# First block's input projections as three single-pass products, with lead-in, expert end and query scaling rearranged

## The chip, the core and the metric

The kernel runs on one core of a Trainium2 chip. The metric is the device time of one execution in microseconds. The engines of the core run side by side, each with its own list of instructions, and wait for each other by semaphores: TensorE (PE in the rows, its weight loads PEld), VectorE (DVE), ScalarE (ACT), GpSimd (POOL), and SyncE (SP), which only issues transfers from memory.

## What is computed

Two blocks of two layers each, over 256 tokens of width 1024, all in float32. Of the reference the first block matters most, cut here to the lines around the change:

```python
h = rmsnorm(x, ln1_g[i]) @ w_in[i]
(fq, fk, fv, ff, dq, dk, dv, c_q, c_kv, k_r) = jnp.split(h, split_points, axis=-1)
o_fox = fox_group(fq, fk, fv, ff, fgate_b[i])
o_diff = diff_group(dq, dk, dv, lam_q1[i], lam_k1[i], lam_q2[i], lam_k2[i], diff_norm_g[i], lam_init)
o_mla = mla_group(c_q, c_kv, k_r, q_norm_g[i], w_uq[i], kv_norm_g[i], w_ukv[i], pos)
x = x + jnp.concatenate([o_fox, o_diff, o_mla], axis=-1) @ w_o[i]
up = causal_dwconv(rmsnorm(x, ln2_g[i]) @ w_up[i], conv_w[i], conv_b[i])
...
q2 = jax.nn.silu(to_heads_2(hq, HGRN_HEADS)) * (HGRN_HEAD_DIM ** -0.5)
...
return jax.vmap(lambda yb, ib: jnp.zeros((s, d), yb.dtype).at[ib.reshape(-1)].add(yb.reshape(-1, d)))(ye, idx)
```

`w_in[i]` is 1024 by 2724. The second block has a mixer of retention and HGRN2 heads (whose queries are `q2`) and sixteen experts of width 1024, and the experts' outputs are added back to their tokens (last line).

## The kernel before, in words

**First block, a layer (loop over `lay`, TensorE from line 1754 on).** The normalised rows are transposed on TensorE (`turn_normed`) into PSUM and copied out to `XT` with the gain. The projection is cut into twelve blocks (`IN_BLOCKS`): `cq`, `ckv`, `dq0`, `dk0`, `dv0`, then `dq1`, `dk1`, `dv1`, `fv`, `ff`, `fq`, `fk`, all 256 columns wide except `ckv` (160: 128 as `tokens_product`, 32 as `columns_product`) and `ff` (4). Each block has two halves of eight products over the 1024 inputs. Weights come from memory through a ring of six slots of 1 MB (`load` at line 747, in the order of use); a slot is given back by `release`, which runs one block late: it waits for the last block's `proj` when the next one is released. Blocks 0 to 4 run with the small latent and MLA products between them. Blocks 5 to 11 stand in a loop of six turns (`n`, `N_SHARED`): half a block, `step(2n)`, half a block, `step(2n+1)`. A step is the scores of one head's unit, the transposes of the unit before and the values of the one before that; between these VectorE adds the bias and takes the minimum (L1373), ScalarE does the exponential (L1015) and copies the transposes (L1022), VectorE scales the outputs (L1385 to L1399).

**The products.** A float32 product of the language is two matrix instructions in the trace. The feed-forward part (`up`, `down`) already works in another way: a weight tile is rounded by ScalarE into `W1` (`split_round`, L726), VectorE writes the remainder into `W2` (`split_rest`, L730), the rows are split likewise into `XT1` and `XT2`, and each product is three instructions of one pass, `W1·XT1`, `W1·XT2`, `W2·XT1` (L1988 to L1990, L2001), with three pairs of buffers. The first two feed-forward tiles are rounded behind the last attention unit. `split_rest` of the second one stands in VectorE's list between the first and the second of the four additions to the residual (L1436). Its slot is that of `fk`, which the late `release` gives back only when the output projection's first slot is released.

**The lead-in.** SyncE issues the load of `X` and of the identity and then waits for all the small parameter rows before it loads weights. ScalarE issues these rows (17 transfers, L949), waits for the lambda dots, issues the first table of constants, loads its function table and then does the squares of the first norm (L602). VectorE does the lambda dots and the parameter copies first, and the second block's lower bounds behind the first transposes. TensorE turns the parameter rows, does 20 idle products on the identity (L1734) and then the transposes and block 0.

**Second block.** `hqT`, the queries of 128 by 1024, is scaled by GpSimd (L872) once both halves are in; GpSimd then does the level exponents (L888, L889), which all levels of the scores need. In the experts, four groups of four, TensorE waits for each quad of weights (L2200). At a group's end ScalarE copies the left half of the outputs, VectorE the right one, and four products (L2238) scatter both halves to the tokens, followed by four additions (L1699) and, behind the last group, the squares of the next norm (L602). Of the last quad the right halves are loaded last.

## Time and profile before

| | us |
|---|---|
| median of 3 runs | 2084.36 (2083.1 to 2088.19) |
| the profiled execution, its own time | 2084.47 |
| its span in the profile | 2082.7 |
| PE busy | 1675.8 (80% of the span) |
| DVE busy | 620.8 (30%) |
| ACT busy | 449.5 (22%) |
| POOL busy | 176.6 (8%) |

The profile is of one execution. The first block's layer 0 lies at 0 to about 374 us, layer 1 up to 734, the second block's layers from there to about 1406 and to the end. The busy shares are means over stages: in the expert stages, from about 970 us and from about 1640 us on, the transfers move 421 GB/s nearly throughout, while in the first block they move at most 241 GB/s in any fortieth up to 728 us.

### The profile page before, as it was taken

The page shows a single profiled execution, that of the slowest core. Times are in us where ns is not written, and L with a number is a line of the kernel's source. Part 1 is how long each engine was busy: PE and PEld are TensorE (multiplying, and loading weights), DVE is VectorE, ACT ScalarE, POOL GpSimd, SP SyncE. Part 2 cuts the span into 40 slices and gives each one's busy share as a digit, 9 for nine tenths or more (in the row PEclk, how much of TensorE's full clock was granted, in tenths as well). Part 3 has the DMA queues.
Part 4 walks back from the last instruction along what each step waited for, and adds up shares of the span by engine and source line. Part 5 has one row for each costly group of instructions (what it writes and reads, how often), then busy time and mean ns, then how long its engine had stood idle before and what let it go on. Part 6 is the DMA issues. An engine that isn't in the chain of part 4 may idle for free.

```text
span 2082.7 us, 24357 instructions
## 1 busy us (share of the span) xinstructions
PE 1675.8 (80%) x10076; PEld 1165.3 (56%) x10076; DVE 620.8 (30%) x1067; ACT 449.5 (22%) x827; POOL 176.6 (8%) x129
## 2 busy tenths in 40 slices
PE   7999999999999999997565656569999665565665
PEld 6788999788899888983121212118888221121211
DVE  1235666232666665522000000006632110000001
ACT  1244544123455442211000000004212000000000
POOL 0010000001000017410000000002731000000000
PEclk9999999999999999998787788789999788788868
DMA  7226555231655573348999999999234899999997
GB/s 241 90 67 203 190 190 179 74 102 47 233 184 190 173 238 112 115 161 340 421 421 421 421 421 421 421 397 287 95 135 198 337 421 422 421 421 422 421 421 281
DMA packets 197426, 559.94 MB, mean 269 GB/s; under 512 B 15240, under 2 KB 137526, under 8 KB 148934
## 3 DMA queue, kind: packets, MB, share of 16 engines
q1 hardware_dynamic: 187616, 549.82, 68.9%
q10 hardware_dynamic: 9702, 8.57, 1.3%
q8 instruction: 82, 1.34, 0.3%
q14 instruction: 26, 0.21, 0.0%
HBM read 557.30 MB, written 1.05 MB: 268 GB/s over the span
## 4 chain that ended last, share of the span: by engine, by line
PE 50%; issue 24%; DMA 16%; DVE 4%; PEld 2%; ACT 2%; POOL 1%; SPq 1%; ACTq 0%; PEldq 0%; DVEq 0%; POOLq 0%; another core or an unknown queue 0%
DMA ring<-in_w_down 9%; PE psum L1749 8%; PE psum L1741 8%; PE psum L2001 5%; PE psum L2200 5%; PE psum L1988 4%; PE psum L1989 4%; PE psum L1990 4%; DMA ring<-in_w_up 4%; DMA ring<-in_w_gate 3%; PE psum L2111 3%; PE psum L2068 2%; PEld psum L1919 1%; PE psum L1869 1%; PE psum L634 1%
## 5 line engine op out<-in xcount | busy, mean ns | idle before, releaser
L2200 PE MATMUL psum<-ring,arena 128*32 128x512 f32 x2960 | 479.1, 798 | 325.4 <-DMA ring<-in_w_down 133.0
L2200 PEld LDWEIGHTS psum<-ring,arena 128*32 128x32 f32 x2960 | 114.2, 140 | 663.7 <-issue 655.1
L1741 PE MATMUL psum<-XT,ring 128*128 128x256 f32 (+1 forms) x1056 | 234.2, 381 | 0.0
L1741 PEld LDWEIGHTS psum<-XT,ring 128*128 128x128 f32 (+1 forms) x1056 | 196.5, 188 | 30.9 <-issue 2.4
L1988 PE MATMUL psum<-XT,W 128*128 128x256 f32 x704 | 200.0, 284 | 0.1
L1989 PE MATMUL psum<-XT,W 128*128 128x256 f32 x704 | 199.4, 283 | 0.0
L1990 PE MATMUL psum<-XT,W 128*128 128x256 f32 x704 | 199.3, 283 | 0.0
L730 DVE TENSOR_TENSOR W<-ring,W 128x2048 fp32r<-128x2048 f32 x66 | 151.2, 2290 | 106.8 <-ACT W L726 106.8
L1749 PE MATMUL psum<-ring,XT 128*128 128x256 f32 (+1 forms) x832 | 177.1, 371 | 0.0
L1749 PEld LDWEIGHTS psum<-ring,XT 128*128 128x128 f32 x832 | 152.1, 190 | 19.9 <-issue 0.8
L1692 DVE TENSOR_TENSOR arena<-arena,psum 128x512 f32<-128x512 f32 x16 | 11.0, 689 | 467.7 <-PE psum L2200 467.7
L726 ACT ACTIVATE W<-ring 128x2048 fp32r<-128x2048 f32 x66 | 124.2, 1908 | 85.0 <-PE psum L1990 58.3
L1988 PEld LDWEIGHTS psum<-XT,W 128*128 128x128 f32 x704 | 134.2, 191 | 1.0 <-DVE XT L707 0.3
L1989 PEld LDWEIGHTS psum<-XT,W 128*128 128x128 f32 x704 | 134.2, 191 | 0.8
L1990 PEld LDWEIGHTS psum<-XT,W 128*128 128x128 f32 x704 | 134.2, 191 | 0.0
L2001 PE MATMUL psum<-W,hT 128*128 128x512 f32 x528 | 128.1, 399 | 4.6 <-DVE hT L1464 4.6
L2001 PEld LDWEIGHTS psum<-W,hT 128*128 128x128 f32 x528 | 100.0, 192 | 26.4 <-DVE hT L1464 5.5
L1694 DVE COPY arena<-psum 128x512 f32<-128x512 f32 x8 | 5.5, 692 | 315.4 <-PE psum L2200 315.4
L621 POOL TENSOR_TENSOR arena<-arena 128x2 f32<-128x2 f32 x8 | 5.6, 697 | 817.1 <-DVE arena L613 817.1
L1454 DVE SCALAR_TENSOR_TENSOR arena<-psum,arena 128x255 f32<-128x255 f32 (+1 forms) x176 | 72.6, 476 | 3.8 <-ACT arena L1083 3.0
L1222 ACT ACTIVATE arena<-psum 128x512 f32<-128x512 f32 x16 | 9.6, 598 | 290.7 <-PE psum L2227 289.7
L1225 ACT ACTIVATE arena<-psum 128x512 f32<-128x512 f32 x8 | 4.8, 598 | 284.1 <-PE psum L2200 284.1
(253 smaller groups left out, 1742.7 us busy)
## 6 DMA issues: line engine op xcount, KB each, us to landing
ring<-in_w_up SPq DMA_DIRECT2D x170, 1024.0 KB, 17.1
ring<-in_w_down SPq DMA_DIRECT2D x142, 1024.0 KB, 19.4
ring<-in_w_gate SPq DMA_DIRECT2D x116, 1024.0 KB, 18.4
ring<-in_w_in SPq DMA_DIRECT2D x56, 1024.0 KB, 6.5
arena<-in_w_gate SPq DMA_DIRECT2D x12, 1024.0 KB, 12.6
ring<-in_w_o SPq DMA_DIRECT2D x8, 1024.0 KB, 5.2
ring<-in_w_out SPq DMA_DIRECT2D x8, 1024.0 KB, 5.2
ring<-in_w_down SPq DMA_DIRECT2D x16, 512.0 KB, 15.3
```

What stands on the lines that cost most here:

```text
L726: nc.scalar.activation(W1[(v - FF_USE) % W_BUFS][:, :], slot(s), ACT.Copy).then_inc(rounded, 1)
L730: nc.vector.tensor_tensor(W2[(v - FF_USE) % W_BUFS][:, :], slot(v % SLOTS_1), W1[(v - FF_USE) % W_BUFS][:, :].bitcast(F32), ALU.subtract). ...
L1454: last = nc.vector.scalar_tensor_tensor(out=dst, in0=psum[:, 4 + 2 * (j % 2) + g, m * S:m * S + S - tap], scalar=par[:, col + c:col + c + ...
L1741: last = nc.tensor.matmul(out, wt[:, k, c0:c0 + m], XT[:, k, :], start=(k == 0), stop=(k == KD - 1))
L1749: last = nc.tensor.matmul(out, XT[:, k, t * P:(t + 1) * P], wt[:, k, c0:c0 + n], start=(k == 0), stop=(k == KD - 1))
L1988: nc.tensor.matmul(dst, w1[:, k, c], XT1[:, k, :], start=(k == 0), stop=False)
L1989: nc.tensor.matmul(dst, w1[:, k, c], XT2[:, k, :], start=False, stop=False)
L1990: last = nc.tensor.matmul(dst, w2[:, k, c], XT1[:, k, :], start=False, stop=(k == KD - 1))
L2001: last = nc.tensor.matmul(psum[:, 2 * t + c, :], a, b[:, m, 512 * c:512 * (c + 1)], start=(j == 0 and m == 0 and b is w1 and a is h1), sto ...
L2068: last = nc.tensor.matmul(psum[:, 2 * (l % 2) + i, h * P:(h + 1) * P], lk[:, h, i * P:(i + 1) * P], lq[:, h, j * P:(j + 1) * P], start=Tru ...
L2111: last = nc.tensor.matmul(psum[:, 4 + i, t * S:(t + 1) * S], XT[:, k, t * P:(t + 1) * P], wt[:, k, :], start=(t == 0 and k == 4), stop=(k ...
L2200: last = nc.tensor.matmul(psum[CAP * e:CAP * (e + 1), bank + c, :], src[:, 2 * pair + k, CAP * e:CAP * (e + 1)], tiles[e][:, k, 512 * c:51 ...
```

## The change

**Projections.** The twelve blocks of both layers are now computed as the feed-forward part already was: `split_round` on ScalarE, `split_rest` on VectorE, and three single-pass products (`tokens_of`, `columns_of`), with two pairs of buffers in turn (`split_pair`). A tile may be rounded once the block two before it is done (`proj`). A slot of the ring is given back at the start of its block (`split_ready`). The 32 rope columns of `ckv` are computed as the last 32 of 96 columns. In layer 1 the first two tiles are split at the end of layer 0.

**Lead-in.** Twelve parameter rows are issued half by SyncE and half by ScalarE; SyncE doesn't wait for them before the weights. ScalarE loads its table first and does the squares as soon as `X` is there; the five lambda rows are issued behind the squares, the table of constants behind the transposes. The lambda and lower bound work moves behind block 4's splits on VectorE. TensorE does no idle products in layer 0.

**Second block.** ScalarE scales each half of the queries itself. In each layer's last expert group ScalarE copies both halves of the outputs; the left half is scattered before TensorE waits for the last weights, and the additions and squares go by halves.

```diff
+SPLIT_IN = 11
+SPLIT_ORDER = list(range(6)) + ["ff"] + list(range(6, SPLIT_IN)) + list(range(FF_USE, USES_1))
+SPLIT_AT = {v: n for n, v in enumerate(SPLIT_ORDER)}
...
+def split_pair(v):
+
+    return v % 2 if v < SPLIT_IN else (v - FF_USE) % 3
...
-            nc.scalar.activation(W1[(v - FF_USE) % W_BUFS][:, :], slot(s), ACT.Copy).then_inc(rounded, 1)
+            elif v >= FF_USE:
+                act.wait_ge(proj, past(proj) + block_of(SPLIT_IN - 1 - (v - FF_USE)) + 1)
+            elif v >= 2:
+                act.wait_ge(proj, past(proj) + block_of(v - 2) + 1)
+            elif past(up_mm):
+                read, k = ((up_mm, 0), (down_mm, 1))[v]
+                act.wait_ge(read, past(read) - k)
+            n = split_width(v)
+            nc.scalar.activation(W1[split_pair(v)][:, 0:n], slot(s, n), ACT.Copy).then_inc(rounded, 1)
...
+            sp.wait_ge(s_zero, 5)
+            for dst, src in parameter_rows()[1::2]:
+                sp.dma_start(dst, src).then_inc(s_rows, 16)
...
-            sp.wait_ge(s_rows, ROWS)
...
-                pool.wait_ge(emp_act, past(emp_act) + 6)
-                pool.tensor_scalar(hqT, hqT, HD ** -0.5, None, ALU.mult).then_inc(hq_scaled, 1)
...
+            nc.scalar.preload_act_table_set(EXP_LN_SET)
+            for dst, src in parameter_rows()[0::2]:
                 act.dma_start(dst, src).then_inc(s_rows, 16)
-            act.wait_ge(s_lamd, 2 * DEPTH)
-            act.dma_start(cst[:, P:], const1[:, P:]).then_inc(s_tables, 16)
-            nc.scalar.preload_act_table_set(EXP_LN_SET)
-            nc.scalar.activation(lame, lams, ACT.Exp).then_inc(s_lame, 1)
+            act.wait_ge(s_small, SMALL)
+            squares(act, BY_ROWS, None, sumsq)
+            for dst, src in lambda_rows():
+                act.dma_start(dst, src).then_inc(s_lamr, 16)
...
+                scale_last_tokens(act, past, 0)
+                act.wait_ge(s_par, 2 * (lay + 1))
                 if lay == 0:
-                    act.wait_ge(par_cur, 1)
-                    squares(act, BY_ROWS, None, sumsq)
-                else:
-                    squares(act, BY_ROWS, lambda i: (x_out, past(x_out) - 3 + i), sumsq)
-                act.wait_ge(par_cur, past(par_cur) + 1)
-                scale_last_tokens(act, past, 0)
-                turn_act(act, past, 0, par[:, C_LN1:C_LN1 + 8])
+                    split_round(act, past, 0)
+                turn_split_act(act, past, 0, 0, par[:, C_LN1:C_LN1 + 8])
+                if lay == 0:
+                    split_round(act, past, 1)
...
+                    act.dma_start(cst[:, P:], const1[:, P:]).then_inc(s_tables, 16)
...
+                split_round(act, past, 2)
...
+                split_round(act, past, 3)
...
+                split_round(act, past, 4)
...
+                split_round(act, past, 5)
+                if lay == 0:
+                    act.wait_ge(s_lamd, 2 * DEPTH)
+                    nc.scalar.activation(lame, lams, ACT.Exp).then_inc(s_lame, 1)
+                    act.wait_ge(set2, 2)
+                    nc.scalar.activation(lb_t[:, 8:16], lb_t[:, 8:16], ACT.Exp).then_inc(set2a, 1)
+                act.wait_ge(wu_loaded, past(wu_loaded) + 48)
+                nc.scalar.activation(wf1[:, :, :], wf, ACT.Copy).then_inc(rounded, 1)
...
+                    if n < N_SHARED - 1:
+                        split_round(act, past, 6 + n)
...
+                if lay < DEPTH - 1:
+                    for v in range(2):
+                        split_round(act, before(lay + 1), v)
...
+                    if name[:2] == "hq":
+                        act.wait_ge(emp_act, past(emp_act) + n + 1)
+                        nc.scalar.activation(dst, dst, ACT.Copy, scale=HD ** -0.5).then_inc(hq_scaled, 1)
...
-                    act.wait_ge(dn_mm, past(dn_mm) + 1)
-                    nc.scalar.activation(YE[:, 0:512], psum[:, 6, :], ACT.Copy).then_inc(ye_ready, 1)
+                    for c in range(2 if g == N_GROUPS - 1 else 1):
+                        act.wait_ge(dn_mm, past(dn_mm) + c + 1)
+                        nc.scalar.activation(YE[:, 512 * c:512 * (c + 1)], psum[:, 6 + c, :], ACT.Copy).then_inc(ye_ready, 1)
...
-                nc.vector.tensor_copy(par, par_all[:, lay, :]).then_inc(par_cur, 1)
-                dve.wait_ge(par_cur, past(par_cur) + 1)
+                par = par_all[:, lay, :]
+                if lay == 0:
+                    dve.wait_ge(s_small, SMALL)
                 norm_dve(dve, past, 0)
-                turn_dve(dve, past, 0, par[:, C_LN1:C_LN1 + 8])
                 if lay == 0:
-                    lower_bounds()
+                    parameters()
+                turn_split_dve(dve, past, 0, 0, par[:, C_LN1:C_LN1 + 8],
+                               (lambda: split_rest(dve, past, 0)) if lay == 0 else None)
+                if lay == 0:
+                    split_rest(dve, past, 1)
+                split_rest(dve, past, 2)
...
+                split_rest(dve, past, 3)
                 dve.wait_ge(latT, past(latT) + 1)
...
+                split_rest(dve, past, 4)
                 copied_by_dve(3, dkT[:, 0:2, :])
...
+                split_rest(dve, past, 5)
+                if lay == 0:
+                    lambdas()
+                    lower_bounds()
+                dve.wait_ge(rounded, past(rounded) + SPLIT_AT["ff"] + 1)
+                nc.vector.tensor_tensor(wf2[:, :, :], wf, wf1[:, :, :].bitcast(F32), ALU.subtract).then_inc(rest, 1)
...
+                    if n < N_SHARED - 1:
+                        split_rest(dve, past, 6 + n)
                     bias_and_max(2 * n)
...
+                    for n, (t, cols, c) in enumerate(BY_ROWS if g < N_GROUPS - 1 else BY_HALVES):
+                        dve.wait_ge(sc_mm, past(sc_mm) + n + 1)
+                        nc.vector.tensor_tensor(X[:, t, cols], psum[:, scatter_bank(g, t, c), :], X[:, t, cols], ALU.add).then_inc(x_moe, 1)
...
-                idle_products(7, IDLE_PRODUCTS["first block"])
+                if lay:
+                    idle_products(7, IDLE_PRODUCTS["first block"])
...
+                def split_ready(v):
+
+                    pe.wait_ge(rest, past(rest) + SPLIT_AT[v] + 1)
+                    pe.sem_inc(slot_free[v % SLOTS_1], 1)
+                    return W1[split_pair(v)][:, :], W2[split_pair(v)][:, :]
+
+                def columns_of(out, w1, w2, c0, m):
+
+                    for k in range(KD):
+                        c = slice(c0, c0 + m)
+                        nc.tensor.matmul(out, w1[:, k, c], XT1[:, k, :], start=(k == 0), stop=False)
+                        nc.tensor.matmul(out, w1[:, k, c], XT2[:, k, :], start=False, stop=False)
+                        last = nc.tensor.matmul(out, w2[:, k, c], XT1[:, k, :], start=False, stop=(k == KD - 1))
+                    return last
+
+                def tokens_of(out, t, w1, w2, n, fresh=False):
+
+                    rows = slice(t * P, (t + 1) * P)
+                    for k in range(KD):
+                        if fresh:
+                            pe.wait_ge(xt_rest, past(xt_rest) + k + 1)
+                        nc.tensor.matmul(out, XT1[:, k, rows], w1[:, k, 0:n], start=(k == 0), stop=False)
+                        nc.tensor.matmul(out, XT1[:, k, rows], w2[:, k, 0:n], start=False, stop=False)
+                        last = nc.tensor.matmul(out, XT2[:, k, rows], w1[:, k, 0:n], start=False, stop=(k == KD - 1))
+                    return last
 
...
-                        last = tokens_product(b[:, half * P:(half + 1) * P], half, wt, 0, KV_RANK)
+                        last = tokens_of(b[:, half * P:(half + 1) * P], half, w1, w2, KV_RANK)
                         if half:
-                            last = columns_product(b[NOPE:MLA_QK, S:2 * S], wt, KV_RANK, ROPE)
+                            last = columns_of(b[0:MLA_QK, S:2 * S], w1, w2, KV_RANK - NOPE, MLA_QK)
...
-                        if name != "ff":
-                            release(proj, past(proj) + i + 1, [use(i) % SLOTS_1])
...
+                                scatter(0, BY_HALVES[:TT])
...
+                    def scatter(half, chunks):
+                        pe.wait_ge(ye_ready, past(ye_ready) + half + 1)
+                        for t, cols, c in chunks:
+                            nc.tensor.matmul(psum[:, scatter_bank(g, t, c), :], GT[:, g, t * P:(t + 1) * P], YE[:, cols],
+                                             start=True, stop=True).then_inc(sc_mm, 1)
...
+                    if g < N_GROUPS - 1:
+                        scatter(1, BY_ROWS)
+                    else:
+                        scatter(1, BY_HALVES[TT:])
```

The lead-in in ScalarE's list: before, the issues are followed by the constants, the table and the squares. (L949 are the parameter and lambda rows, L951 the constants, L602 the squares, L609 the scaling of the last tokens, L663 the transposed rows.)

```order
L949 DMA arena<-in_lam_q 128x2x64
L949 DMA arena<-in_lam_k 128x2x64
L949 DMA arena<-in_lam_q 128x2x64
L949 DMA arena<-in_lam_k 128x2x64
L951 DMA arena<-first_constants 128x2912
L952 ACT_TABLE_LOAD
L953 ACTIVATE arena<-arena 128x4
L602 ACTIVATE XN,arena<-X 128x512 x4
L609 ACTIVATE XN<-X,arena 128x512 x2
L663 ACTIVATE XT<-psum,arena 128x256 x4
```

And in the changed kernel (L645 squares, L995 lambda rows, L652 scaling, L779 the rounding, L737 the rows' first parts):

```order
L991 DMA arena<-in_fgate_b 1x2x4
L991 DMA arena<-in_norm_g 8x2x128
L645 ACTIVATE XN,arena<-X 128x512 x4
L995 DMA arena<-in_diff_norm_g 128x2x128
L995 DMA arena<-in_lam_q 128x2x64
L995 DMA arena<-in_lam_k 128x2x64
L995 DMA arena<-in_lam_q 128x2x64
L995 DMA arena<-in_lam_k 128x2x64
L652 ACTIVATE XN<-X,arena 128x512 x2
L765 ISA
L779 ACTIVATE W_0_49<-ring 128x2048
L737 ACTIVATE XT_55<-psum,arena 128x256 x6
```

The table and half of the rows stand ahead of the squares, the five lambda rows between squares and scaling, and the rounding of the first tile ahead of the turned rows' first parts.

VectorE between block 1 and the MLA copies, before (L1309, L1312 and L1314 empty the latents and the rope columns, L1317 and L1321 are the turned latents, L1305 the copy of `dk0`):

```order
L1309 TENSOR_SCALAR arena<-psum,arena 128x256 x2
L1312 TENSOR_SCALAR arena<-psum,arena 128x128 x2
L1314 COPY arena<-psum 32x256
L1317 TENSOR_TENSOR arena<-psum,arena 128x512
L1321 TENSOR_SCALAR arena<-psum,arena 128x256
L1305 COPY arena<-psum 128x512
L1327 COPY arena<-psum 64x512 x2
```

And in the changed kernel (L784 is `split_rest`, L1382 to L1387 the latents and the rope columns, L1391 and L1395 the turned latents, L1378 the copy of `dk0`):

```order
L784 TENSOR_TENSOR W_0_52<-ring,W_0_49 128x2048
L1382 TENSOR_SCALAR arena<-psum,arena 128x256 x2
L1385 TENSOR_SCALAR arena<-psum,arena 128x128 x2
L1387 COPY arena<-psum 32x256
L784 TENSOR_TENSOR W_1_53<-ring,W_1_50 128x2048
L1391 TENSOR_TENSOR arena<-psum,arena 128x512
L1395 TENSOR_SCALAR arena<-psum,arena 128x256
L784 TENSOR_TENSOR W_0_52<-ring,W_0_49 128x2048
L1378 COPY arena<-psum 128x512
L1402 COPY arena<-psum 64x512 x2
```

The remainder of the tile of `dk0` now stands behind the latents, whose squares wait for block 1, and that of `dv0` behind the turned latents.

GpSimd in the second block's mixer, before (L869 limits the forget terms, L872 scales the queries, L888 and L889 are the exponents of the first level):

```order
L869 TENSOR_SCALAR arena<-arena 128x512 x4
L872 TENSOR_SCALAR arena<-arena 128x1024
L888 TENSOR_TENSOR arena<-arena 128x4x128
L889 TENSOR_TENSOR arena<-arena 128x4x128
L888 TENSOR_TENSOR arena<-arena 128x8x64
```

And in the changed kernel:

```order
L927 TENSOR_SCALAR arena<-arena 128x512 x4
L943 TENSOR_TENSOR arena<-arena 128x4x128
L944 TENSOR_TENSOR arena<-arena 128x4x128
L943 TENSOR_TENSOR arena<-arena 128x8x64
L944 TENSOR_TENSOR arena<-arena 128x8x64
```

The scaling is gone from the list, and the exponents follow at once.

## Rows read from the trace of the kernel before

**Rows 1.** The page: the span, and the chain that ended last by engine.

```profile
span 2082.7 us, 24357 instructions
PE 50%; issue 24%; DMA 16%; DVE 4%; PEld 2%; ACT 2%; POOL 1%; SPq 1%; ACTq 0%; PEldq 0%; DVEq 0%; POOLq 0%; another core or an unknown queue 0%
```

**Rows 2.** Windows: stretch, length, busy us (count) per engine, clock, DMA share, GB/s.

```profile
68.00:150.00 82.00, 81.32 (x445) 66.94 (x444) 27.33 (x112) 29.17 (x105) 6.38 (x6) 1.00 0.27 81
```

**Rows 3.** Timeline, lead-in: start, us, engine, line, operation, tiles, count, [idle before].

```profile
13.45 6.81 PE L1734 MATMUL psum<-arena 128*128 128x128 f32 x40
17.34 0.63 ACT L602 ACTIVATE XN<-X 128x512 f32<-128x512 f32 x1 [1.75 <-DVE arena L1296]
23.76 10.64 PE L1749 MATMUL psum<-ring,XT 128*128 128x256 f32 x64
34.33 10.74 PE L1741 MATMUL psum<-XT,ring 128*32 128x256 f32 x48
```

**Rows 4.** DMA issues (KB, us to landing); one issue on ScalarE in the timeline.

```profile
X<-in_x SPq DMA_DIRECT2D x1, 1024.0 KB, 4.9
...
8.97 0.49 ACTq L949 DMA_DIRECT2D arena<-in_lam_k  x1
```

**Rows 5.** Timeline: neighbouring single-pass products; chain of waits: 24 products 512 wide.

```profile
185.18 0.28 PE L1990 MATMUL psum<-XT,W 128*128 128x256 f32 x1
185.30 0.28 PE L1988 MATMUL psum<-XT,W 128*128 128x256 f32 x1
...
205.26 5.49 PE psum L2001 x24
```

**Rows 6.** The page's groups: line, operation, count | busy, mean ns | idle.

```profile
L730 DVE TENSOR_TENSOR W<-ring,W 128x2048 fp32r<-128x2048 f32 x66 | 151.2, 2290 | 106.8 <-ACT W L726 106.8
L726 ACT ACTIVATE W<-ring 128x2048 fp32r<-128x2048 f32 x66 | 124.2, 1908 | 85.0 <-PE psum L1990 58.3
```

**Rows 7.** Timeline, third and fourth block of layer 0 and the latents between them.

```profile
38.41 0.28 ACT L989 ACTIVATE arena<-psum 128x128 f32<-128x128 f32 x1
41.94 0.42 DVE L1314 COPY arena<-psum 32x256 f32<-32x256 f32 x1
45.57 7.07 PE L1741 MATMUL psum<-XT,ring 128*128 128x256 f32 x32
```

**Rows 8.** Timeline, attention steps of layer 0: two half blocks one step apart.

```profile
77.55 3.62 PE L1741 MATMUL psum<-XT,ring 128*128 128x256 f32 x16
83.00 3.62 PE L1741 MATMUL psum<-XT,ring 128*128 128x256 f32 x16
```

**Rows 9.** Timeline, from the output projection to the second norm, layer 0.

```profile
163.78 9.66 PE L1919 MATMUL psum<-ring,XT 128*128 128x256 f32 x44
164.88 5.66 SPq L752 DMA_DIRECT2D ring<-in_w_up  x3
172.00 2.29 DVE L730 TENSOR_TENSOR W<-ring,W 128x2048 fp32r<-128x2048 f32 x1 [3.01 <-ACT W L726]
177.90 0.16 DVE L613 TENSOR_REDUCE arena<-arena 128x2 f32<-128x10 f32 x1 [1.82 <-ACT XN L602]
```

**Rows 10.** Timeline, second block's mixer, layer 0, around the query scaling.

```profile
785.01 0.69 DVE L1557 TENSOR_TENSOR arena<-arena 128x512 f32<-128x512 f32 x1
785.15 3.18 POOL L872 TENSOR_SCALAR arena<-arena 128x1024 f32<-128x1024 f32 x1 [8.80 <-ACT arena L1148]
796.49 3.56 PE L2068 MATMUL psum<-arena 128*128 128x128 f32 x16 [5.14 <-POOL arena L896]
```

**Rows 11.** Timeline, the end of the last expert group.

```profile
2066.12 3.54 PE L2200 MATMUL psum<-ring,arena 128*32 128x512 f32 x16 [3.12 <-DMA ring<-in_w_down]
2070.57 3.71 PE L2238 MATMUL psum<-arena 128*128 128x512 f32 x8 [0.90 <-DVE arena L1694]
2075.04 0.63 ACT L602 ACTIVATE XN<-X 128x512 f32<-128x512 f32 x1
```

**Rows 12.** Timeline, last down projection of layer 0's feed-forward part.

```profile
366.17 7.42 PE L2001 MATMUL psum<-W,hT 128*128 128x512 f32 x24 [2.31 <-DVE hT L1464]
```

265 lines of the change are left out of this document (136 added, 129 removed).

## Prediction

> **What bounds the kernel now.** The page's chain gives TensorE half of the span and transfers 16% [rows 1]; the windows say where. In the attention loop of layer 0 TensorE is busy 81.3 of 82 us, VectorE 27.3 and ScalarE 29.2 [rows 2]. So the first block is TensorE's, with room on the two engines that would split the weights. The expert stages wait for transfers and are not touched but at their ends; what the stages ahead save moves them forward unchanged. I therefore read the timeline of the first block product by product, and then each place where the change moves something.
>
> **Price of a product.** A whole block of 256 columns is 16 products, 32 instructions in 7.07 us [rows 7]; the last one's tail overlaps, so it takes about 6.9, a half about 3.45. Single-pass instructions start 0.12 us apart [rows 5], so a block will be 48 x 0.12 = 5.76. Gain 1.14 for each of ten blocks. `ff` has 8 products and gains 0.57.
>
> `ckv` is open. Before, cq and ckv's 128-column products take 10.64 together [rows 3], so these take 3.57, or 0.22 a product; with the 32 rope columns (3.45) 7.0. After, the rope part costs 24 x 0.12 = 2.9. No row shows a single-pass product 128 wide. From below: 24 products 512 wide take 5.49 [rows 5], 0.229 each, so 256 columns more cost 0.109, and 128 less would give 0.066. From above: as much as the whole float32 product of that width, 0.22. I take 0.12, that of the nearest row of its kind, since the same 128x128 weights are loaded for each. Then the block is 48 x 0.12 + 2.9 = 8.6, a loss of 1.6; the ends are 6.1 (gain 0.9) and 13.5 (loss 6.5). The Trainium skill's page TensorE: Matmul & The Clock Gate, section LDWEIGHTS, has a load take columns/1.2 ns, 107 ns for 128; by it the block would be about 8.0. No row shows a load alone.
>
> **Splitting, where it lies.** A tile costs ScalarE 1.91 and VectorE 2.29 [rows 6]. *In the loop*, a turn is two half blocks and two steps; the half blocks start 5.45 apart [rows 8], so a turn is 10.9 before and 10.9 - 1.14 = 9.8 after. Before, ScalarE is busy 29.17/82 of it and VectorE 27.33/82 [rows 2], 3.9 and 3.6 a turn; with the splits [rows 6] it is 5.8 and 5.9 of 9.8. More than the sums count the places. I laid the two lists against TensorE's (an estimate, to some 0.5): rounding ends 3.4 into the turn, the remainder at 5.7, two bias operations and the exponential of unit 2n at 7.8, and its transposes are due at 8.5. So nothing waits, by 0.7. The turn of `ff` adds the forget gate to ScalarE ahead of the rounding: I count 0.8 lost. Five turns: 5 x 1.14 + 0.57 - 0.8 = 5.5 gained a layer.
>
> *At the fourth block* it is on the path. Its tile can be rounded only when block 1 is done (two pairs), the latents' squares follow, GpSimd's power, VectorE's latents, and only then stands its `split_rest`. Chain from block 1's end: rounding 1.9, from the squares to the end of VectorE's rope copy 42.36 - 38.0 = 4.4 [rows 7], remainder 2.3, with handovers 8.8. Block 2 and the latents' transposes are 5.8 + 1.0. So block 3 starts about 2 us late, and from block 0's end to its own end there are 8.6 + 8.8 + 5.8 = 23.2, against (45.57 - 30.9) + 6.9 = 21.6: a loss of 1.6 a layer, against 1.1 that the sum of products alone would give. With the ends for `ckv` it is a gain of 0.9 or a loss of 6.5.
>
> *From there to the loop's second turn* block 4 and block 5 gain 2.3. In layer 0 the lambda work and the lower bounds (some 5 us of small operations with two waits on ScalarE) now stand on VectorE between block 5's remainder and the MLA rotations; with the next remainder behind them the first bias comes late, and I count 1.7 of waiting: gain 0.6 there, 2.3 in layer 1. Block 0 of layer 1 gains 1.0; its tiles are split behind the last down projection, 7.42 us on TensorE [rows 12], which hides 3.1 and 3.7 us; without it they would cost that.
>
> **Second norm.** Before, `fk`'s slot comes back at 164.88, the weight lands 5 us later, is rounded and its remainder ends at 174.3, with three additions behind it; the sums are reduced at 177.90 [rows 9]. Given back at `fk`'s start, the tile is there long before. Next late is TensorE: its last product ends at 173.4 [rows 9]; addition, squares and handover bring the reduction to 175.3. Gain 2.6 a layer.
>
> **Lead-in.** The squares start at 17.34, block 0 at 23.76, ends at 30.9 [rows 3]. `X` lands 4.9 after its issue [rows 4], so the squares run from 6.2 to 8.7. Five issues of 0.49 [rows 4] hold ScalarE until 11.2; scaling ends at 12.6, the rounding of tile 0 at 14.6 (its load is issued near 5 and lands at 10 to 12), remainder at 17.1, where block 0 starts. TensorE has done nothing but transposes. Before, its first 20-odd idle instructions ran at half pace: 40 took 6.81 against 0.11 each later [rows 3], so some 2.4 us were lost where nothing waited. Now that loss falls on block 0: end 17.1 + 5.8 + 2.3 = 25.2. Gain 5.5, between 3 and 7. The Trainium skill's page TensorE: Matmul & The Clock Gate, section PE-mode transpose, says that transposes don't bring the full clock; that speaks against dropping the idle products, and the 2.3 stand with or without it.
>
> **Query scaling.** GpSimd's 3.18 delays the first exponents; they could start at 785.7 behind VectorE's last key instead of 788.4, and TensorE waits 5.14 for what follows [rows 10]. Gain 2.6 in each of two layers. ScalarE's two scalings lie under the blocks that TensorE still has.
>
> **Expert end.** The last weights land at 2066.12, scatter starts at 2070.57, the last square at 2075.04 [rows 11]. The left half's copy, scatter and addition now fit into TensorE's wait before 2066.12. Behind the last weights two scatters and two additions are left: last square at about 73.3. Gain 1.75, twice.
>
> **Sum.** Lead-in 5.5. Layer 0: -1.6 + 0.6 + 5.5 + 2.6 = 7.1. Layer 1: 1.0 - 1.6 + 2.3 + 5.5 + 2.6 = 9.8. Scaling 5.2, expert ends 3.5. Together 31.1. One price more: where TensorE waited 2.31 before the last down projection, 24 products took 7.42 instead of 5.49 [rows 12], 1.9 lost. There are three or four new waits of about 2 us; I take one such loss, 2 us. Gain 29. The profiled execution's own time is 2084.47, 1.8 over its span and 0.1 over the median 2084.36: 2084.5 - 29 = **2055.5**.
>
> **Rivals.**
> - *Narrow products at the float32 price* (0.22): 4.9 more a layer, and no wait of block 3 hides it, since its chain begins at block 1's end. 2055.5 + 9.8 = 2065. For it: half of the float32 cost here is columns, and nothing shows the single-pass form keeping its pace below 256. Against: 512 and 256 lie on one line.
> - *Narrow products at 0.066*: 2.5 less a layer, 2050.5.
> - *The lead-in doesn't move*: if tile 0 lands late behind `X` and the rows, or the cold start lasts longer, its 5.5 are gone: 2061.
> - *Slower: the splits end on the path in the loop.* If ScalarE and VectorE can't run ahead of TensorE, each of twelve turns shows 1.91 + 2.29 = 4.2: 50 us, 2106. It decides at 29/12 = 2.4 exposed per turn; I find 0.7 us of room instead, and VectorE is a third busy today [rows 2]. Partly exposed, at 2 us a turn, it would be 2080, about no change.
>
> **Chances.** Main case (2051 to 2060) 0.45; narrow products at 0.22 (2061 to 2070) 0.32; at 0.066 (2046 to 2051) 0.1; lead-in not moved, alone, 0.06; no change 0.04; slower 0.03. The range 2047 to 2069 leaves out under 2 in 10. A measurement here tells 0.3% (6 us) from no change: faster 0.93, same 0.04, slower 0.03.
>
> **What would show it.** Right: block 0's first product near 17 and its end near 25; single-pass products 0.12 apart in all blocks; TensorE waiting 2 us before block 3 and none in the loop; the reduction of the second norm 2 behind the output projection; GpSimd's exponents right behind the last key; one copy and two scatters behind the last weights. Wrong: ckv's 48 narrow products taking 10 us and not 6; a wait on `split_rest` in any turn; block 0 later than 19. The forecast falls if the loop's turn is not near 9.8.

## The result and the profile after the change

The changed kernel takes 2038.21 us (median of 4 runs, 2036.06 to 2038.32) against 2083.83 (4 runs, 2083.1 to 2088.19): 0.9774 of the time before, 95% interval 0.9757 to 0.9791. That is 46 us less, where I had forecast 29: the direction was right, the gain was more than half as large again, and 2038 lies under the range's lower end of 2047.

The page of the profile after answers to [rows 1]: span, busy times, chain by engine.

```profile
span 2036.3 us, 25114 instructions
...
PE 1644.7 (81%) x10420; PEld 1158.6 (57%) x10420; DVE 678.1 (33%) x1103; ACT 492.1 (24%) x861; POOL 175.4 (9%) x127
...
PE 45%; issue 24%; DMA 17%; PEld 6%; DVE 5%; ACT 2%; POOL 1%; SPq 1%; PEldq 0%; ACTq 0%; DVEq 0%; POOLq 0%; another core or an unknown queue 0%
```

TensorE's share of the chain fell from 50% to 45% of a shorter span, with 10420 instructions instead of 10076: more instructions, but shorter ones. VectorE is busy 33% of the span (30 before) and ScalarE 24% (22): the price of splitting, and it lies beside TensorE's work.

I followed the same instruction through both traces, place by place. "Ahead" is before minus after; "gained" is what the stretch up to that place adds to it; the last column is the term that the prediction had for it.

| place | before | after | ahead | gained | forecast |
|---|---|---|---|---|---|
| block 1 starts (end of lead-in and block 0) | 30.8 | 23.2 | 7.6 | 7.6 | 5.5 |
| block 3 done, MLA products start | 52.5 | 45.9 | 6.6 | -1.0 | -1.6 |
| loop's second turn starts | 77.6 | 69.7 | 7.9 | 1.4 | 0.6 |
| first unit behind the loop | 134.7 | 120.0 | 14.6 | 6.7 | 5.5 |
| second norm turned, first feed-forward product | 181.7 | 164.4 | 17.3 | 2.7 | 2.6 |
| layer 1: block 0 starts | 380.7 | 363.5 | 17.2 | -0.1 | 0 |
| block 3 done | 409.4 | 392.3 | 17.1 | -0.1 | -0.6 |
| loop's second turn starts | 434.5 | 414.9 | 19.5 | 2.4 | 2.3 |
| turning the mixed heads behind the loop | 494.2 | 467.9 | 26.3 | 6.7 | 5.5 |
| second norm turned | 539.4 | 509.7 | 29.8 | 3.5 | 2.6 |
| mixer of layer 0: first product | 743.0 | 713.4 | 29.6 | -0.2 | 0 |
| first level scores | 796.5 | 763.2 | 33.3 | 3.7 | 2.6 |
| behind the levels | 893.8 | 859.3 | 34.5 | 1.2 | 0 |
| last 16 expert products of layer 0 | 1396.9 | 1362.7 | 34.1 | -0.4 | 0 |
| mixer of layer 1: first product | 1410.4 | 1372.9 | 37.5 | 3.4 | 1.75 |
| first level scores | 1463.8 | 1423.1 | 40.7 | 3.2 | 2.6 |
| behind the levels | 1561.9 | 1519.2 | 42.8 | 2.1 | 0 |
| last 16 expert products of layer 1 | 2066.1 | 2023.2 | 42.9 | 0.1 | 0 |
| reduction of the last norm | 2075.9 | 2029.5 | 46.4 | 3.5 | 1.75 |

The forecast terms add up to 31.1, the measured ones to 46.4; the forecast then took off 2 us for a slower clock behind new waits, of which this profile shows nothing. So 17.3 us were missing, and they are spread: some 5 in the mixers, 3.4 at the expert ends, 2.1 in the lead-in, 2.4 in the two loops, 2 that were not lost, and smaller ones.

**Lead-in.** Timeline of the changed kernel (start, us, engine, line, operation, tiles, count, idle before); it answers to [rows 3, 4].

```profile
6.17 0.63 ACT L645 ACTIVATE XN<-X 128x512 f32<-128x512 f32 x1 [3.27 <-DMA arena<-first_constants]
6.19 0.41 ACTq L995 DMA_DIRECT2D arena<-in_diff_norm_g  x1
...
8.38 0.51 ACTq L995 DMA_DIRECT2D arena<-in_lam_k  x1
...
9.88 1.34 ACT L652 ACTIVATE XN<-X,arena 128x512 f32<-128x512 f32 x2 [1.16 <-POOL arena L664]
...
10.74 3.65 PE L677 MATMUL psum<-arena,XN 128*128 128x128 f32 x16 [1.20 <-ACT XN L652]
11.66 1.91 ACT L779 ACTIVATE W<-ring 128x2048 fp32r<-128x2048 f32 x1 [0.45 <-DMA ring<-in_w_in]
...
13.61 2.29 DVE L784 TENSOR_TENSOR W<-ring,W 128x2048 fp32r<-128x2048 f32 x1
...
16.00 0.55 PE L1868 MATMUL psum<-W,XT 128*128 128x256 f32 x1 [1.61 <-issue]
...
23.19 0.22 PE L1868 MATMUL psum<-W,XT 128*128 128x128 f32 x1
```

The squares stand at 6.17 as I expected. The five lambda issues are on ScalarE's queue from 6.19 to 8.9, beside its squares and not ahead of its next work. So the scaling starts at 9.88, when GpSimd's power is there, and the chain goes on with the rounding at 11.66 (it waits 0.45 for the tile's load) and the remainder at 13.61. Block 0 starts at 16.00 and is done at 23.19.

**The narrow products and the fourth block.** Timeline, TensorE, end of block 1 to block 3; it answers to [rows 3, 7].

```profile
28.39 0.28 PE L1870 MATMUL psum<-W,XT 128*128 128x128 f32 x1
28.50 0.30 PE L1857 MATMUL psum<-XT,W 128*96 128x256 f32 x1
...
31.36 0.28 PE L1857 MATMUL psum<-XT,W 128*128 128x256 f32 x1
...
37.70 0.67 PE L1907 MATMUL psum<-arena 128*128 128x128 f32 x4 [0.44 <-DVE arena L1387]
...
40.11 0.36 PE L1857 MATMUL psum<-XT,W 128*128 128x256 f32 x1 [1.53 <-DVE W L784]
```

From 23.19 to 28.50 stand the 48 single-pass products (one instruction each) with 128 moving columns: 0.111 each. The rope part takes 28.50 to 31.36, 2.9. Block 1 takes 8.2. Block 3 waits 1.53 for VectorE's remainder (L784).

**The loop.** Windows (stretch, length, busy us and count of PE, PEld, DVE, ACT, POOL, then clock, DMA share, GB/s): three turns of layer 1.

```profile
414.93:444.17 29.24, 29.24 (x226) 26.45 (x224) 15.81 (x47) 14.37 (x35) 0.00 (x0) 1.00 0.31 106
```

A turn is 29.24 / 3 = 9.75 us against 10.9 [rows 8], TensorE is never idle in it, VectorE is busy 5.3 us of it and ScalarE 4.8.

**The waits that are left, and the second norm.** Timeline, TensorE: the first exponential of layer 0's loop, and the transposes of the second norm in both layers.

```profile
69.38 0.52 PE L1989 MATMUL psum<-arena 128*128 128x128 f32 x3 [1.02 <-ACT arena L1069]
...
162.44 1.96 PE L677 MATMUL psum<-arena,XN 128*128 128x128 f32 x16 [0.55 <-ACT XN L652]
...
507.72 1.96 PE L677 MATMUL psum<-arena,XN 128*128 128x128 f32 x16 [0.55 <-ACT XN L652]
```

The same transposes in the kernel before:

```profile
179.74 1.94 PE L634 MATMUL psum<-arena,XN 128*128 128x128 f32 x16 [3.24 <-ACT XN L609]
...
536.30 3.14 PE L634 MATMUL psum<-arena,XN 128*128 128x128 f32 x16 [2.88 <-ACT XN L609]
```

The waits of 3.24 and 2.88 became 0.55. In layer 1 the 16 transposes also went from 3.14 to 1.96; in layer 0 they took 1.94 before, behind the longer wait.

**Query scaling.** Timeline of the mixer of layer 0, which answers to [rows 10].

```profile
753.03 0.68 DVE L1620 TENSOR_TENSOR_SCAN arena<-arena 128x255 f32<-128x255 f32 x1
...
753.79 1.54 POOL L943 TENSOR_TENSOR arena<-arena 128x512 f32<-128x512 f32 x1 [7.63 <-DVE arena L1620]
...
757.26 1.53 DVE L1643 TENSOR_TENSOR arena<-arena 128x512 f32<-128x512 f32 x1
...
763.22 2.05 PE L2172 MATMUL psum<-arena 128*128 128x128 f32 x16 [1.46 <-POOL arena L951]
```

GpSimd's first exponents (L943) start right behind VectorE's last scan at 753.03, and run beside the VectorE exponents that I had taken for its last key. They take 1.5 us each where they took 1.04 (the line below is of the kernel before), and VectorE's own exponents (L1643, 1.53 instead of 0.69), which now run at the same time, are longer too. TensorE waits 1.46 instead of 5.14, and its 16 level scores take 2.05 instead of 3.56.

```profile
788.41 1.04 POOL L888 TENSOR_TENSOR arena<-arena 128x512 f32<-128x512 f32 x1
```

**Expert end.** Timeline of the end of the last group, which answers to [rows 11].

```profile
2020.73 1.99 PE L2320 MATMUL psum<-arena 128*128 128x512 f32 x4 [0.71 <-ACT arena L1288]
...
2023.19 1.92 PE L2305 MATMUL psum<-ring,arena 128*32 128x512 f32 x16 [0.47 <-DMA ring<-in_w_down]
...
2025.91 1.99 PE L2320 MATMUL psum<-arena 128*128 128x512 f32 x4 [0.80 <-ACT arena L1288]
...
2029.47 0.16 DVE L1562 TENSOR_REDUCE arena<-arena 128x2 f32<-128x6 f32 x1 [0.86 <-ACT XN L645]
```

Two of the four scatter products (four of their eight instructions) stand in the wait for the last weights. TensorE waits 0.47 instead of 3.12, and the 16 products behind take 1.92 instead of 3.54.

### The profile page after: what moved, and what is told of

Same layout as the page of the kernel before. It is cut to its first block, busy times and chain, and to the rows that moved or that the text cites. A ratio compares the mean times of both kernels' runs of the same rounds, so it can differ in the third digit from the quotient of the medians.

```text
span 2036.3 us, 25114 instructions
## 1 busy us (share of the span) xinstructions
PE 1644.7 (81%) x10420; PEld 1158.6 (57%) x10420; DVE 678.1 (33%) x1103; ACT 492.1 (24%) x861; POOL 175.4 (9%) x127
## 3 DMA queue, kind: packets, MB, share of 16 engines
q10 hardware_dynamic: 9440, 8.46, 1.3%
## 4 chain that ended last, share of the span: by engine, by line
PE 45%; issue 24%; DMA 17%; PEld 6%; DVE 5%; ACT 2%; POOL 1%; SPq 1%; PEldq 0%; ACTq 0%; DVEq 0%; POOLq 0%; another core or an unknown queue 0%
DMA ring<-in_w_down 9%; PE psum L1834 5%; PE psum L2305 5%; PE psum L1826 4%; DMA ring<-in_w_gate 3%; DMA ring<-in_w_up 3%; PE psum L2105 3%; PE psum L2029 3%; PE psum L2215 3%; PE psum L2092 2%; PE psum L2094 2%; PE psum L2093 2%; PE psum L2172 2%; PEld psum L2105 2%; PEld psum L2094 2%
## 5 line engine op out<-in xcount | busy, mean ns | idle before, releaser
L784 DVE TENSOR_TENSOR W<-ring,W 128x2048 fp32r<-128x2048 f32 x88 | 199.8, 2272 | 137.3 <-ACT W L779 137.1
L779 ACT ACTIVATE W<-ring 128x2048 fp32r<-128x2048 f32 x88 | 164.6, 1893 | 80.5 <-PE psum L2094 58.1
L1826 PE MATMUL psum<-XT,ring 128*128 128x256 f32 x640 | 139.4, 379 | 0.0
L1826 PEld LDWEIGHTS psum<-XT,ring 128*128 128x128 f32 x640 | 121.0, 190 | 16.1
L1834 PE MATMUL psum<-ring,XT 128*128 128x256 f32 x512 | 112.5, 379 | 0.0
L1834 PEld LDWEIGHTS psum<-ring,XT 128*128 128x128 f32 x512 | 96.9, 190 | 13.1
```

The source lines that it names most:

```text
L779: nc.scalar.activation(W1[split_pair(v)][:, 0:n], slot(s, n), ACT.Copy).then_inc(rounded, 1)
L784: nc.vector.tensor_tensor(W2[split_pair(v)][:, 0:n], slot(v % SLOTS_1, n), W1[split_pair(v)][:, 0:n].bitcast(F32), ALU.subtract).then_inc( ...
L1826: last = nc.tensor.matmul(out, wt[:, k, c0:c0 + m], XT[:, k, :], start=(k == 0), stop=(k == KD - 1))
L1834: last = nc.tensor.matmul(out, XT[:, k, t * P:(t + 1) * P], wt[:, k, c0:c0 + n], start=(k == 0), stop=(k == KD - 1))
```

## Experiments

My theory after the comparison: the mechanisms were those of the prediction, but I had priced a wait at its length alone. Behind a long wait TensorE runs its next few microseconds at half its clock; a wait that is shortened or filled gives that back as well. The rival: each part simply gave more than its term, for reasons of its own. How often the half clock follows a wait is counted over all traces behind the last experiment. The first four kernels put that to the test on the kernel before; a gain in us is the ratio's distance from 1 times 2084.

### Idle products in three waits of the kernel before

```diff
-"feed-forward": 12
+"feed-forward": 24
...
 if last_quad and (k, c) == (0, 1):
+    idle_products(3, 12)
     pe.wait_ge(late_loaded, layer_past(late_loaded) + 16 * (1 + GROUP))
...
 def level(l):
+    if l == 0:
+        idle_products(3, 22)
     pe.wait_ge(mul_pool, past(mul_pool) + l + 1)
```

> The kernel before, with nothing of the change: only products whose result nobody reads are put into three of TensorE's waits, 22 before each second block's first level scores, 12 more before the second norm's transposes, 12 before the last 16 expert products of a layer. Theory of pace (formed on the trace after the change: half of what I had not forecast is TensorE running at half pace behind a long wait, and a shortened wait gives that back on top of itself): the level scores go from 3.6 to about 1.9 us and layer 2's next products from 7.5 to 6.9, the transposes of the second norm in layer 1 from 3.14 to 1.95, the 16 expert products from 3.54 to 1.92; each wait ends when it ended before. In all 1.6 x 2 + 1.6 + 2.2 + 1.2 = about 8 us less than before (2076). Pricing of my prediction, in which a wait costs its length alone: no change (2084). Rival: the idle products delay what stands behind them: slower, 2086 or more.

Measured 2074.35 us against 2085.57, ratio 0.9945 (0.9933 to 0.9957): 11.5 us gained by instructions that compute nothing. Timeline, TensorE, at three of the places:

```profile
536.34 1.94 PE L634 MATMUL psum<-arena,XN 128*128 128x128 f32 x16 [0.21 <-ACT XN L609]
...
793.71 2.05 PE L2070 MATMUL psum<-arena 128*128 128x128 f32 x16
...
1392.95 1.92 PE L2203 MATMUL psum<-ring,arena 128*32 128x512 f32 x16
```

The transposes of layer 1's second norm take 1.94 (3.14 before), the level scores 2.05 (3.56), the 16 expert products 1.92 (3.54 [rows 11]). Windows over those 16 products, of this kernel and then of the kernel before:

```profile
1392.80:1395.00 2.20, 2.00 (x17) 0.42 (x16) 0.00 (x0) 0.00 (x0) 0.00 (x0) 1.00 1.10 349
```

```profile
1396.80:1400.40 3.60, 3.54 (x16) 0.59 (x16) 0.00 (x0) 0.00 (x0) 0.00 (x0) 0.53 1.10 347
```

The same 16 instructions: at a granted clock of 1.00, the upper level (2.4 GHz), here, at 0.53, nearly the lower one (1.2 GHz) throughout, in the kernel before. The five places give 1.2 + 1.5 + 1.6 + 2.4 + 1.6 = 8.3. Another 1.6 came where I had changed nothing: the last down projection of layer 1 took 5.78 instead of 7.37 behind the same wait of 2.31. The last pair of runs returns to that.

### The query scaling alone, on the kernel before

```diff
-pool.wait_ge(emp_act, past(emp_act) + 6)
-pool.tensor_scalar(hqT, hqT, HD ** -0.5, None, ALU.mult).then_inc(hq_scaled, 1)
...
+if name[:2] == "hq":
+    act.wait_ge(emp_act, past(emp_act) + n + 1)
+    nc.scalar.activation(dst, dst, ACT.Copy, scale=HD ** -0.5).then_inc(hq_scaled, 1)
```

> The kernel before with the query scaling alone moved from GpSimd to ScalarE. My prediction's term: 2.6 a layer, 5.2 in all (2079). Theory from the traces: GpSimd's first exponents depend on the sums alone and start 5.2 us earlier, but then share the time with VectorE's and take 1.5 instead of 1.04 each, which leaves 3.2 to 3.8 for the wait; and TensorE's level scores behind the shorter wait run at full pace, 1.2 to 2.1 more: together 5 a layer, 10 in all (2074). If the scaling is not the cause, the gain stays at or under 5.

Measured 2076.55 against 2085.57, ratio 0.9951 (0.9938 to 0.9965): 10.2 us (7 to 13). My 5.2 lies outside. Timeline, the first level scores of both layers:

```profile
790.52 2.05 PE L2069 MATMUL psum<-arena 128*128 128x128 f32 x16 [1.59 <-POOL arena L894]
...
1451.57 2.05 PE L2069 MATMUL psum<-arena 128*128 128x128 f32 x16 [1.41 <-POOL arena L894]
```

Waits of 1.59 and 1.41 instead of 5.14 and 5.00, and 2.05 for the 16 products instead of 3.56 and 3.79.

### The expert end alone, on the kernel before

```diff
 if last_quad and (k, c) == (0, 1):
+    scatter(0, BY_HALVES[:TT])
     pe.wait_ge(late_loaded, layer_past(late_loaded) + 16 * (1 + GROUP))
...
-act.wait_ge(dn_mm, past(dn_mm) + 1)
-nc.scalar.activation(YE[:, 0:512], psum[:, 6, :], ACT.Copy).then_inc(ye_ready, 1)
+for c in range(2 if g == N_GROUPS - 1 else 1):
+    act.wait_ge(dn_mm, past(dn_mm) + c + 1)
+    nc.scalar.activation(YE[:, 512 * c:512 * (c + 1)], psum[:, 6 + c, :], ACT.Copy).then_inc(ye_ready, 1)
```

> The kernel before with the end of the last expert group alone as in the changed kernel (left half copied, scattered and added before the last weights, ScalarE copies both halves). My prediction's term: 1.75 twice, 3.5 in all (2080.5). Theory of pace: four scatter products stand in the wait, so the 16 products behind it take 1.92 instead of 3.54, together 3.4 twice, 6.9 in all (2077).

Measured 2078.75 against 2085.57, ratio 0.9965 (0.9952 to 0.9978): 7.3 us (4.6 to 10.0). My 3.5 lies outside, the 6.9 of the theory inside. Timeline, TensorE, the last group:

```profile
2060.82 1.99 PE L2221 MATMUL psum<-arena 128*128 128x512 f32 x4 [0.71 <-ACT arena L1231]
2063.32 1.92 PE L2206 MATMUL psum<-ring,arena 128*32 128x512 f32 x16 [0.51 <-DMA ring<-in_w_down]
```

### The early return of a slot alone, on the kernel before

```diff
 j = 2 * N_SHARED
 step(j)
+release(None, 0, [])
 pe.wait_ge(free_dve, past(free_dve) + IN_COUNT[11])
```

> The kernel before, where TensorE gives the last projection's slot back right behind the block instead of behind the output projection. Nothing else is changed. My prediction's term: 2.6 a layer, 5.2 in all (2079); by the theory of pace the transposes of layer 1's second norm also go from 3.14 to 1.96, which makes about 6.3 (2078). If the load was not what the second norm waited for, or if the early transfer delays those of the output weights, no gain (2084).

Measured 2077.82 against 2085.57, ratio 0.996 (0.9948 to 0.9972): 8.3 us (5.8 to 10.8). My 5.2 lies just outside, the 6.3 of the theory inside. TensorE's waits before the second norm's transposes fell from 3.24 and 2.88 to 0.93 and 0.54 us, and layer 1's transposes from 3.14 to 1.94. That is the mechanism of the forecast: the weight behind `fk`'s slot was what the norm waited for. The trace holds 2.3 + 3.5 for it. The 1.2 of the second term need not belong to the shorter wait: the profile of the query scaling alone, where nothing of this is changed, shows the same transposes at full pace behind a wait of 2.86:

```profile
536.54 1.94 PE L634 MATMUL psum<-arena,XN 128*128 128x128 f32 x16 [2.86 <-ACT XN L609]
```

And one of the last down projections, here layer 0's, was 1.6 faster by itself (5.77 for 7.42), while the lead-in of this execution was 1.8 slower by itself. Its span is 5.4 us shorter than that of the profile before; how the 8.3 of the medians are made up beyond the trace's 5.8 stays open.

### The first block alone: the changed kernel without scaling and expert end

```diff
+pool.wait_ge(emp_act, past(emp_act) + 6)
+pool.tensor_scalar(hqT, hqT, HD ** -0.5, None, ALU.mult).then_inc(hq_scaled, 1)
...
-scatter(0, BY_HALVES[:TT])
```

> The changed kernel with two of its parts taken back: the query scaling stands on GpSimd again, and the last expert group ends as before. What stays is the first block (single-pass products, their splits, the lead-in, the early return of slots). If the parts add up, the two cost what they gave alone, 10 and 7 us: 2055, and the first block's part is 29 us, where my prediction's terms for it (5.5 + 7.1 + 9.8 = 22.4, less 2 for the clock) say 20, which would be 2064. If much of the gain came from parts that help one another, it is above 2058.

Measured 2055.38 against 2084.5, ratio 0.9864 (0.9851 to 0.9876): 28.4 us. Exactly the 2055 of parts that add up. So the first block with its lead-in is worth 28 and not 20; the two parts taken back, 18.

### The three side edits together, on the kernel before

The diffs of the three single kernels above, together; the projections and the lead-in stay as before.

> The kernel before with the three side edits together and the projections untouched: scaling on ScalarE, new expert end, early return of the last projection's slot. Alone they gave 10, 7 and 8 us. If they add up 2059, and what is left for single-pass projections with the new lead-in is 21 of the 46 us; by the terms of my prediction the three are worth 14 (2070.5) and the projections with the lead-in 17.

Measured 2060.02 against 2084.77, ratio 0.9881 (0.9868 to 0.9895): 24.8 us. Their single gains, 10.2 + 7.3 + 8.3 = 25.8, add up within the intervals. More than half of the 46 us therefore comes from three edits that touch no projection; some 21 are left for the single-pass projections with their lead-in. Of these 7.6 are the lead-in by the table, and 14 the projections (16 by the table's stretches).

### Each remainder in the loop made twice, and three times

These two price the rival on the slower side: how far are VectorE's splits from the path?

```diff
 if n < N_SHARED - 1:
-    split_rest(dve, past, 6 + n)
+    v = 6 + n
+    dve.wait_ge(rounded, past(rounded) + SPLIT_AT[v] + 1)
+    m = split_width(v)
+    nc.vector.tensor_tensor(W2[split_pair(v)][:, 0:m], slot(v % SLOTS_1, m), W1[split_pair(v)][:, 0:m].bitcast(F32),
+                            ALU.subtract).then_inc(twice, 1)
+    n_twice[0] += 1
+    dve.wait_ge(twice, n_twice[0])
+    split_rest(dve, past, v)
```

> The changed kernel, where VectorE makes each remainder of the attention loop's first five turns twice (2.35 us more a turn, the same result). My prediction found 0.7 us of room in a turn: 1.65 exposed, ten times, 16 us slower than the changed kernel (2055). The trace shows more: the first unit's exponential ends some 2.1 us before TensorE wants it, so 0.3 a turn, 3 us slower (2041).

> The same with each remainder made three times (4.7 us more a turn). By the prediction's room of 0.7: 4.0 exposed a turn, ten times, 2078. By the trace's 2.1: 2.6 a turn, 26 us, 2064. VectorE would then be busy some 10 us of a turn of 9.74, so that it bounds the turn as well.

Measured 2050.46 (ratio 0.9839, 0.9826 to 0.9852) and 2076.3 (0.9968, 0.9958 to 0.9979): 12 and 38 us slower than the changed kernel's 2038. Neither number of mine is right: 16 and 40 would follow from 0.7 of room, 3 and 26 from 2.1. Timeline, TensorE, with the remainders doubled: layer 0's first turn, a middle one, and the one behind `ff`.

```profile
70.46 0.87 PE L1999 MATMUL psum<-arena 128*128 128x128 f32 x3 [3.35 <-ACT arena L1070]
...
92.22 0.55 PE L1999 MATMUL psum<-arena 128*128 128x128 f32 x3 [0.41 <-ACT arena L1070]
...
116.45 0.55 PE L1999 MATMUL psum<-arena 128*128 128x128 f32 x3 [1.96 <-ACT arena L1070]
```

The room is not the same in each turn. Of 2.35 us more, 0.41 shows in a middle turn (room 1.9), 1.96 in the turn behind `ff` (room 0.4), and in layer 0's first turn all of it, 3.35 against 1.02 before. And there the half clock comes back. Window over the 24 products behind that wait:

```profile
70.90:76.30 5.40, 5.40 (x28) 5.27 (x26) 2.39 (x2) 2.94 (x6) 0.00 (x0) 0.52 0.60 194
```

They take 5.36 instead of 3.11, at a clock of 0.52. With remainders made three times the waits are up to 5.7 us, and VectorE is busy 10.1 us of a middle turn of 12.4, more than the changed kernel's whole turn of 9.75. So the slower rival was near. In some turns VectorE has more room than the 0.7 that I had counted, in others less or none, and beyond it a microsecond costs more than a microsecond: from twice to three times VectorE has 23.5 us more to do, and the kernel takes 26 more.

### Four waits of the changed kernel treated

```diff
+split_rest(dve, past, 3)
 dve.wait_ge(lat_rms, past(lat_rms) + 1)
...
-split_rest(dve, past, 3)
 dve.wait_ge(latT, past(latT) + 1)
...
-if n < N_SHARED - 1:
+if 0 < n < N_SHARED - 1:
     split_rest(dve, past, 6 + n)
 bias_and_max(2 * n)
+if n == 0:
+    split_rest(dve, past, 6)
...
+for _ in range(6):
+    nc.tensor.matmul(psum[:, 3, 0:P], ident, ident, start=True, stop=True)
 pe.wait_ge(s_rows, ROWS)
...
-if lay:
-    idle_products(7, IDLE_PRODUCTS["first block"])
+idle_products(7 if lay else 3, IDLE_PRODUCTS["first block"] if lay else 4)
...
 pe.wait_ge(s_par, 2 * DEPTH)
+if lay == 0:
+    idle_products(7, 7)
...
+if j == FF_STEPS - 1:
+    idle_products(6, 9)
```

> The changed kernel with four of its waits treated, each readable at its place. (a) VectorE makes the fourth block's remainder before the latents' normalisation, in 2.3 us in which it stands idle: by my theory the wait of 1.53 before block 3 goes in both layers, 3.0 us; if the chain of the latents is what decides, nothing. (b) In the loop's first turn the first unit's bias stands ahead of the next tile's remainder: the wait of 1.0 in layer 0 goes; if the lambda work were the cause and not the order, nothing. (c) 6, 4 and 7 idle products in TensorE's waits of the lead-in: block 0 takes 5.8 instead of 7.25, up to 1.4 us. (d) 9 idle products before the last down projection: its 24 products take 5.5 to 5.8 instead of 7.4, 1.7 a layer, if the pace behind the wait is the cause. Together 8 to 9 us: 2030. By the pricing of my prediction (c) is worth 2.3 and (d) 1.9 a layer.

Measured 2033.23 against 2084.5, ratio 0.9756 (0.9744 to 0.9769): 5 us under the changed kernel's 2038, where I had expected 8 to 9. The four places one by one:

(a) *Miss.* Block 3 starts 16.6 us behind block 1's start instead of 16.9: 0.3 gained, not 1.5. The wait for the remainder is gone, and one of 1.88 for the latents stands there. GpSimd's first operation on the latents in the changed kernel:

```profile
34.21 0.19 POOL L886 TENSOR_SCALAR arena<-arena 128x2 f32<-128x2 f32 x1 [24.36 <-ACT arena L1034]
```

and in this kernel, VectorE, GpSimd and TensorE:

```profile
32.22 2.29 DVE L784 TENSOR_TENSOR W<-ring,W 128x2048 fp32r<-128x2048 f32 x1 [5.87 <-ACT W L779]
...
32.93 1.63 POOL L886 TENSOR_SCALAR arena<-arena 128x2 f32<-128x2 f32 x1 [23.09 <-ACT arena L1034]
...
37.86 0.66 PE L1912 MATMUL psum<-arena 128*128 128x128 f32 x4 [1.88 <-DVE arena L1388]
```

GpSimd's 0.19 us became 1.63: it ends at 34.56, just behind VectorE's remainder (34.51). The room on VectorE was there, but its use held GpSimd: the latents' last copy on VectorE now ends 15.9 us behind block 1's start instead of 14.5. So the chain lost the remainder and grew by the same 1.4 that GpSimd's operation grew by. The Trainium skill's page SBUF — State Buffer, section SBUF: two separate sides, says that a VectorE operation with two inputs in SBUF and one of GpSimd exclude each other for the whole instruction; the trace agrees.

(b) *Hit.* The wait of 1.02 is gone, and the second turn starts 28.5 us behind block 3 instead of 29.5. It took two things together: the lambda work made VectorE late, and the order put the next tile's remainder (2.29) ahead of the first bias. In layer 1 of the changed kernel the same order stands without the lambda work, and TensorE has no wait at this place.

(c) *Hit.* Timeline, TensorE, lead-in of this kernel:

```profile
6.18 2.93 PE L1797 MATMUL psum<-arena 128*128 128x128 f32 x12 [6.18 <-DMA arena<-first_constants]
...
10.74 1.97 PE L677 MATMUL psum<-arena,XN 128*128 128x128 f32 x16 [0.27 <-ACT XN L652]
...
16.09 0.36 PE L1871 MATMUL psum<-W,XT 128*128 128x256 f32 x1 [1.82 <-DVE W L784]
```

The transposes take 1.97 instead of 3.65, block 0 takes 5.82 instead of 7.19. The Trainium skill's page TensorE: Matmul & The Clock Gate, section PE-mode transpose, has it that transposes don't bring the full clock; that agrees: 20 of them from 8.46 on left the array slow until 19.1, with a wait of 1.6 between them and block 0, and products from 6.18 on had it at full pace at 10.74. But the waits of 1.2 and 1.6 around the transposes were filled too, and no run tells the two apart. The loss without idle products was 1.4, not 2.3.

(d) *Hit at its place:* the last down projections take 5.77 in both layers instead of 7.38 and 7.42. But see the next run.

### The changed kernel again, and three of the four waits

The second is the kernel above with (a) as in the changed kernel.

> The changed kernel itself, on the chip of these runs, as the base for the kernels with three and four waits treated: 2038, and by the traces they stand 6 to 7 us below it.

> The kernel of the four waits without (a): the fourth block's remainder stands behind the latents again, as in the changed kernel. The trace of the four waits showed that moving it only put a wait of 1.88 for the latents in the place of 1.53 + 0.44, because GpSimd's first small operation took 1.63 us instead of 0.19 beside VectorE's remainder. So this should be 0.3 a layer slower than the four waits, 0.7 in all, which is under what can be measured; if (a) was worth its 1.5 a layer after all, it is 3 slower.

Measured 2036.98 (ratio 0.9769, 0.9756 to 0.9783) and 2034.27 (0.9757, 0.9743 to 0.977), before 2084.77. The kernels with three and with four waits treated can't be told apart, as expected, and stand 3 to 4 us under the changed one, where the traces promised 6 or 7; their intervals overlap with its own. Two things in the profiled executions bear on what is missing. The first is in two executions of one and the same program. Timeline and window over layer 0's last down projection, first in the profile of the changed kernel:

```profile
348.85 7.38 PE L2105 MATMUL psum<-W,hT 128*128 128x512 f32 x24 [2.31 <-DVE hT L1547]
```

```profile
348.80:356.30 7.50, 7.45 (x27) 6.02 (x28) 3.72 (x3) 2.23 (x2) 0.00 (x0) 0.77 0.01 2
```

and in that of the same kernel here:

```profile
349.70 5.80 PE L2105 MATMUL psum<-W,hT 128*128 128x512 f32 x24 [2.31 <-DVE hT L1547]
```

```profile
349.60:355.60 6.00, 5.90 (x27) 4.88 (x28) 3.80 (x4) 2.29 (x2) 0.00 (x0) 1.00 0.01 3
```

The same wait of 2.31, the same 24 products, 7.38 at a clock of 0.77 in one execution and 5.80 at 1.00 in the other. Layer 1 shows the same pair (7.42 and 5.78). So whether a wait of this length costs 1.6 us more is not fixed by the kernel. The idle products of (d) only make sure of what some executions have anyway. The Trainium skill's page TensorE: Matmul & The Clock Gate, section Part 1: The HAM clock gate, says of the start of a kernel that the number of slow products varies from run to run of the same kernel; these rows show the like in its middle.

The second is the wait that the change itself brought, 1.53 us before block 3. In the profile of the changed kernel nothing behind it is slow. In that of the kernel with three waits treated, where it is as long, the block's 48 products take 7.47 and 7.46 us in the two layers instead of 5.99 and 5.98. Windows over block 3 of layer 0, of the changed kernel and of this one:

```profile
40.10:46.10 6.00, 5.99 (x49) 6.00 (x50) 3.18 (x3) 0.00 (x0) 0.00 (x0) 1.00 0.75 242
```

```profile
39.30:46.80 7.50, 7.49 (x49) 7.48 (x50) 3.17 (x3) 0.00 (x0) 0.00 (x0) 0.77 0.65 211
```

So a wait has a price that comes in some executions and not in others. All thirteen profiles together (before, changed, and the eleven kernels of the experiments), with each place where such a wait stands:

| what runs behind the wait | wait | slow in | it takes, slow | it takes, full pace |
|---|---|---|---|---|
| first 16 level scores | 4.8 to 5.3 | 8 of 8 | 3.5 to 3.8 | 2.05 |
| last 16 expert products of a layer | 2.7 to 3.4 | 7 of 8 | 2.7 to 3.6 | 1.92 |
| last down projection | 2.3 | 12 of 22 | 7.2 to 7.4 | 5.8 |
| second norm's transposes, layer 1 | 2.9 | 2 of 3 | 3.1 to 3.2 | 1.94 |
| second norm's transposes, layer 0 | 3.2 to 3.3 | 0 of 3 | | 1.94 |
| block 3 of the changed kernel | 1.5 | 4 of 12 | 7.4 to 7.5 | 5.99 |

Behind waits of up to 1.8 us the level scores, and behind waits of up to 0.7 us the last expert products, run at full pace in every profile. That is the ground for taking the pace as part of what the query scaling and the expert end gave. For the other places a single profile says little.

## Why the prediction was right or wrong

**What bounds the kernel.** Right. The first block was TensorE's, and what was saved ahead of the expert stages moved them forward unchanged: 34.5 us ahead behind the levels and 34.1 at the end of layer 0's experts.

**Price of a product.** Right. Blocks of 256 columns take 5.8, a half block and a turn are as forecast (9.75 for 9.8).

**`ckv`.** Right. 0.111 a product, against 0.12 taken, and the rivals' 0.22 and 0.066; block 1 took 8.2 for 8.6. The load time of the Trainium skill's page TensorE: Matmul & The Clock Gate, section LDWEIGHTS, by which I had 8.0, was closer than the nearest row that I used. The nearest row of all was in my own working: the 32 float32 instructions of that width take 3.57, 0.11 each, the price that came; I divided by products of two instructions and so gave the high rival 0.32. Both high and low price fall.

**The fourth block.** Right in kind, the size off by 0.5: TensorE waits 1.53 for VectorE's remainder, and -1.0 stands against -1.6 in layer 0. The attempt to take the remainder out of the chain made the latents' part longer by 1.4, through GpSimd, so it gained 0.3.

**From there to the second turn.** Right in layer 1 (2.4 for 2.3). In layer 0 I counted 1.7 of waiting, and 1.02 came; it takes the lambda work and the order on VectorE together, as experiment (b) and layer 1 show.

**The loop.** 6.7 for 5.5 in each layer. The mis-sized term is the turn of `ff`: I took off 0.8 for the forget gate, and no wait shows there; `ff` itself took 2.83 instead of 3.55. The room of 0.7 per turn is no property of the turn: in place it is some 2, 0.4 or nothing.

**Second norm.** Right in layer 0 (2.7 for 2.6). In layer 1 it gave 3.5: the transposes ran at full clock, which one of three profiles with the old wait shows as well, so that part may be luck of the execution.

**Lead-in.** 7.6 for 5.5. Two terms were off. I let five issues of 0.49 hold ScalarE until 11.2; they ran beside its squares, and the start of block 0 came at 16.0 for 17.1. And block 0 lost 1.4 to the slow start, not 2.3.

**Query scaling.** 5 a layer for 2.6: the largest miss. The step that failed is "they could start at 785.7 behind VectorE's last key": the row at 785.01 is no key but VectorE's own half of the same exponents (L1557). GpSimd's exponents follow the last scan, at 783.2 in the kernel before, so they came 5.2 us earlier, and lost 1.8 of that again beside VectorE (four of 1.5 for 1.04). That makes 3.2 to 3.8 for the wait. The rest, 1.2 and 2.1, is TensorE's pace behind it. I had the row for it, 3.56 for 16 products [rows 10] with 1.95 for the same 16 later in that trace, and did not ask why it was long.

**Expert end.** 3.4 for 1.75, twice. The rearrangement gave exactly 1.75 + 0.1; the missing 1.6 is the half clock of 16 products, 3.54 [rows 11], which I had taken as their price.

**The clock.** The second step that failed. I priced new waits with the slow stretch behind them, one loss of 2 us, and did not price the old waits of 2.9 to 5 us that the change shortens, each with a slow stretch of its own: 1.2 + 2.1 behind the level scores, 2 x 1.6 at the expert ends, 0.9 at layer 1's second norm. With the 2 us taken off that is 9.4 of the 17.3 that were missing. Of these the 6.5 of the level scores and expert ends stand in nearly every profile (15 of 16 places), and the idle products in the kernel before show the pace as a cause and not only as company. The 0.9 and the 2 are partly luck: in the profile of the changed kernel the new waits of 1.53 and 1.02 have nothing slow behind them, but behind the wait of 1.53 the slow stretch came in 4 of 12 places, at 1.5 us each. By that count its two places cost 1 us on average (an estimate), and taking nothing off would not have been right either. Its size was misread as well: 7.42 is of the timeline and 5.49 of the chain of waits; like with like, 7.4 against 5.8, the loss is 1.6 and not 1.9.

**Rivals.** The narrow products at either end, the lead-in that stays, and no change are refuted by the rows above. The slower one did not come, but the doubled remainders show that it stood only 0.4 to 1.9 us of VectorE's work a turn away, and nothing in layer 0's first turn.

## What to carry to other kernels

Price a wait with what runs behind it: compare the same group of instructions behind the wait and elsewhere (3.54 and 1.92 for 16 products here), and count the difference as part of what shortening the wait gives. Look at the same place in several executions before the difference is counted in full: here it came every time behind waits of 5 us, about every other time behind 2.3, and one time in three behind 1.5. Room on an engine is to be counted in each turn and not as a mean, and with what its use holds up elsewhere. Compare durations of one view only: the same kind of 24 products is 5.49 in the chain of waits and 5.8 in the timeline. When a change has several parts, measure the small ones by themselves: here three edits of a few lines gave 25 of 46 us, and the rewriting of twelve projections some 14 to 16.

## What the hardware showed that I had not expected

- Of one and the same program and the same wait of 2.31 us, one execution ran the next 24 products in 7.38 us and another in 5.80. In the kernel before, the 16 transposes behind a wait of 3.24 in layer 0 took 1.94 and those behind 2.88 in layer 1 took 3.14. With doubled remainders the first products behind a wait of 1.96 took 4.22 for 3.11. The wait of 1.53 before block 3 had a slow stretch behind it in 4 of 12 places (7.4 to 7.5 for 5.99), the one of 2.31 before the last down projection in 12 of 22.
- A small GpSimd operation took 1.63 us instead of 0.19 beside a VectorE subtraction of 2.29; two-input operations of 512 columns took 1.5 on both engines when they ran together, instead of 1.04 and 0.69.
- Transfers issued on ScalarE's queue while it computes did not delay its activations: five issues from 6.19 to 8.9 beside four squares and the four reads of their sums. The scaling behind them was not due before 9.88.
- A single-pass product of 128 moving columns costs 0.111 us, hardly less than one of 256 (0.12), behind the same load of 128 weights.
